# Feed-forward inner rows turned by 32x32 blocks on VectorE and gathered by transfers, in a two-block transformer kernel

## The reference

```python
def swiglu(h, w_gu, w_down):
    g, u = jnp.split(h @ w_gu, 2, axis=-1)
    return (jax.nn.silu(g) * u) @ w_down
```

## Time and profile before

| | us |
|---|---|
| median of three runs (1355.02 to 1355.81) | 1355.55 |
| span of the profiled execution, first to last instruction | 1354.2 |
| PE busy in it | 1339.0 |
| DVE busy | 930.6 |
| ACT busy | 749.4 |
| POOL busy | 67.2 |

### The profile page before, as it was taken

The page is one execution under the profiler, slowest core; times in us unless marked ns, Lnnn a source line. Parts: engine busy times, 40 slices in busy tenths (PEclk is TensorE's granted clock), DMA queues, the critical chain, the costliest instruction groups (busy, mean ns, idle before and its releaser), DMA issues.

```text
span 1354.2 us, 17190 instructions
## 1 busy us (share of the span) xinstructions
PE 1339.0 (99%) x6599; PEld 1117.7 (83%) x6599; DVE 930.6 (69%) x1334; ACT 749.4 (55%) x1169; POOL 67.2 (5%) x132
## 2 busy tenths in 40 slices
PE   9999999999999999999999999999999999999998
PEld 6888888888888888888788888889988888788886
DVE  6677867856656777877767787678866455755553
ACT  6444448567864544446845444766457664744442
POOL 3100100000000000010000010100000000000000
PEclk9999999999999999999999999999999999999999
DMA  9888866543376678885577885665544355556662
GB/s 282 290 262 277 310 199 190 167 117 108 100 243 195 214 252 272 289 288 167 168 245 250 279 290 150 202 173 159 168 140 112 108 172 169 166 180 184 187 190 88
DMA packets 167057, 270.89 MB, mean 200 GB/s; under 512 B 14242, under 2 KB 114826, under 8 KB 166976
## 3 DMA queue, kind: packets, MB, share of 16 engines
q1 hardware_dynamic: 154240, 226.66, 53.8%
q0 software_dynamic: 12576, 43.06, 9.5%
q10 hardware_dynamic: 160, 0.07, 0.0%
HBM read 268.66 MB, written 1.05 MB: 199 GB/s over the span
## 4 chain that ended last, share of the span: by engine, by line
PE 94%; DVE 3%; ACT 1%; DMA 1%; issue 0%; POOL 0%; DVEq 0%; SPq 0%; ACTq 0%
PE ps L1982 25%; PE ps L1947 16%; PE ps L1949 16%; PE ps L1948 16%; PE ps L2171 2%; PE ps L1961 1%; PE ps L2182 1%; PE ps L1962 1%; PE ps L1963 1%; PE ps L2065 1%; PE ps L2067 1%; PE ps L2066 1%; PE ps L2488 1%; PE ps L1997 1%; PE ps L2086 1%; PE ps L2255 1%
## 5 line engine op out<-in xcount | busy, mean ns | idle before, releaser
L1151 DVE TENSOR_TENSOR w_lo<-raw,w_hi 128x1024 fp32r<-128x1024 f32 (+2 forms) x431 | 515.1, 1214 | 249.1 <-ACT w_hi L636 246.9
L636 ACT ACTIVATE w_hi<-raw 128x1024 fp32r<-128x1024 f32 (+2 forms) x431 | 448.5, 1054 | 330.5 <-DMA raw<-in_ffn_wgu_dram 92.8
L1947 PE MATMUL ps<-w_hi,a_hi 128*128 128x512 f32 (+1 forms) x976 | 390.5, 400 | 1.1 <-DVE w_lo L1151 0.8
L1949 PE MATMUL ps<-w_hi,a_lo 128*128 128x512 f32 (+1 forms) x976 | 379.5, 389 | 0.0
L1948 PE MATMUL ps<-w_lo,a_hi 128*128 128x512 f32 (+1 forms) x976 | 378.5, 388 | 0.0
L1949 PEld LDWEIGHTS ps<-w_hi,a_lo 128*128 128x128 f32 x976 | 183.3, 188 | 38.8
L1947 PEld LDWEIGHTS ps<-w_hi,a_hi 128*128 128x128 f32 x976 | 183.6, 188 | 36.1 <-DVE w_lo L1151 1.0
L1948 PEld LDWEIGHTS ps<-w_lo,a_hi 128*128 128x128 f32 x976 | 183.8, 188 | 34.6
L1982 PE MATMUL ps<-w_hi,hid_hi 128*128 128x512 f32 x300 | 93.5, 393 | 0.0
L1982 PE MATMUL ps<-w_lo,hid_hi 128*128 128x512 f32 x300 | 92.5, 390 | 0.0
L1982 PE MATMUL ps<-w_hi,hid_lo 128*128 128x512 f32 x300 | 92.5, 390 | 0.0
(11 more groups left out here) (433 smaller groups left out, 1640.4 us busy)
## 6 DMA issues: line engine op xcount, KB each, us to landing
raw<-in_ffn_wgu_dram SPq DMA_DIRECT2D x176, 256.0 KB, 4.2
raw<-in_w_in_dram SPq DMA_DIRECT2D x88, 512.0 KB, 3.7
raw<-in_w_gu_dram SPq DMA_DIRECT2D x176, 256.0 KB, 3.3
ada<-in_w_ada_dram POOLq DMA_DIRECT2D x72, 512.0 KB, 5.4
raw<-in_ffn_wdown_dram SPq DMA_DIRECT2D x44, 512.0 KB, 4.6
raw<-in_w_dn_dram SPq DMA_DIRECT2D x44, 512.0 KB, 4.3
raw<-in_w_in_dram SPq DMA_DIRECT2D x36, 256.0 KB, 3.1
raw<-in_w_out_dram SPq DMA_DIRECT2D x16, 512.0 KB, 4.1
```

The source lines that it names most:

```text
L636: act.activation(w_hi[:, u % RING, 0:nk * n], raw[:, u % RING, 0:nk * n], ACT.Copy).then_inc(hi_ready, 1)
L1151: dve.tensor_tensor(w_lo[:, u % RING, 0:nk * n], raw[:, u % RING, 0:nk * n], w_hi[:, u % RING, 0:nk * n].bitcast(F32), ALU.subtract).then_ ...
L1947: pe.matmul(dst(t)[:, 0:n], a[0], slot(u, w_hi, kk, n), start=kc == 0, stop=False)
L1949: i = pe.matmul(dst(t)[:, 0:n], a[1], slot(u, w_hi, kk, n), start=False, stop=kc == KC - 1)
```

## The change

The four PE transposes of a block and their PSUM banks are gone. In their place three steps stand.

- DVE, right after it has made `hid` of a block (now one buffer, not two), transposes it within squares of 32x32 into a new tile `turned_blocks` (`turn_blocks`, two instructions of 128x256).
- After every second block SP issues 16 transfers from SBUF to SBUF, of 32 partitions x 2 x 128 floats (32 KB) each, which bring the squares to their partitions in `gathered` (`gather_hidden`). They stand in the queue that loads the weights, ahead of unit 4j+8 of the block j that comes next, and SP first waits there until both blocks are turned. A feed-forward part has 11 blocks, so there are 6 groups; the last one is for one block, with 16 transfers of half the size.
- ACT and DVE make `hid_hi` and `hid_lo` of two blocks at once from `gathered` (128x1024), after their units up to 4j+9 and just before the silu or `hid` of the even block j.

The diff, cut to its core:

```diff
+            def gather_hidden(f, m):
+
+                nh = 2 * min(2, UPB - 2 * m)
+                g = HGROUPS * f + m
+                sp.wait_ge(sem("blocks_turned"), f * UPB + min(2 * m + 2, UPB))
+                if g >= 1:
+                    sp.wait_ge(sem("hid_lo_ready"), g)
+                for i in range(4):
+                    for q in range(4):
+                        sp.dma_start(gathered[32 * q:32 * q + 32, :, i, 0:nh, :], turned_blocks[32 * i:32 * i + 32, :, q, 0:nh, :])\
+                          .then_inc(sem("hid_gathered"), 16)
+
+            gather_at = {}
+            for f in range(4):
+                for m in range(HGROUPS):
+                    gather_at[ffn[f][0] + 4 * min(2 * m + 2, UPB) + RING] = (f, m)
...
             for u in range(XQ, NU):
+                if u in gather_at:
+                    gather_hidden(*gather_at[u])
                 load_unit(u)
...
-                    if j >= 1:
-                        hidden_hi(f, j - 1)
                     if j < UPB - 1:
                         w.to(up + 4 * j + 8)
+                    if j >= 2 and j % 2 == 0:
+                        hidden_hi(f, j // 2 - 1)
...
-                w.to(dn + 5)
-                hidden_hi(f, UPB - 1)
+                w.to(dn + 8)
+                hidden_hi(f, HGROUPS - 1)
...
+            def hidden_hi(f, m):
+                n = 2 * min(2, UPB - 2 * m)
+                act.wait_ge(sem("hid_gathered"), 256 * (HGROUPS * f + m + 1))
+                act.activation(hid_hi[:, 4 * m:4 * m + n, :].rearrange("p c (g u) -> p c g u", u=32),
+                               gathered[:, :, :, 0:n, :].rearrange("p t i c u -> p c (t i) u"), ACT.Copy).then_inc(sem("hid_hi_ready"), 1)
...
+            def turn_blocks(f, j):
+
+                c = 2 * (j % 2)
+                dve.wait_ge(sem("hid_ready"), f * UPB + j + 1)
+                if j % 2 == 0 and f + j > 0:
+                    dve.wait_ge(sem("hid_gathered"), 256 * (HGROUPS * f + j // 2))
+                for t in range(T):
+                    i = dve.transpose(turned_blocks[:, t, :, c:c + 2, :], hid[:, t, :].rearrange("p (c q u) -> p q c u", c=2, u=32))
+                i.then_inc(sem("blocks_turned"), 1)
...
-            def turn_hidden(f, j):
-                pe.wait_ge(sem("hid_ready"), f * UPB + j + 1)
-                if j >= 2:
-                    pe.wait_ge(sem("hid_lo_ready"), f * UPB + j - 1)
-                for c in range(2):
-                    for t in range(T):
-                        i = pe.transpose(ps[:, 4 + j % 2, c * S + t * P:c * S + (t + 1) * P], hid[:, j % 2, t, c * P:(c + 1) * P], ident)
-                i.then_inc(sem("hid_turned"), 1)
```

More of the change, by code:

```diff
@@ L219, in two_blocks @@
         sg, _, e = place("sg", [P, 2, T, HALF], F32, HB)
-        hid, _, END = place("hid", [P, 2, T, HALF], F32, e)
+        hid, _, e = place("hid", [P, T, HALF], F32, e)
+        turned_blocks, _, END = place("turned_blocks", [P, T, 4, 4, 32], F32, e)
+        gathered, _, _ = place("gathered", [P, T, 4, 4, 32], F32, KD0)
         assert END <= nc.sbuf_usable_end, (END, nc.sbuf_usable_end)
@@ L417, in two_blocks @@
         FFN = ["f0", "f1", "f2", "f3"]
+        HGROUPS = (UPB + 1) // 2
         ROOTS = ["f2_1", "f2_post0", "mix2_0", "f2_post1", "mix2_1", "gla",
@@ L1390, in ffn_part @@
                 w.to(dn + 5)
-                hidden_lo(f, UPB - 1)
                 for n in range(4):
@@ L1395, in ffn_part @@
                     w.to(dn + 8 + 3 * n)
+                    if n == 0:
+                        hidden_lo(f, HGROUPS - 1)
                     if n == 1:
@@ L1402, in ffn_part, with hidden_lo @@
                 w.to(dn + FC + (1 if f == 2 else 2))
-            def hidden_lo(f, j):
-                dve.wait_ge(sem("hid_hi_ready"), f * UPB + j + 1)
-                dst, hf = (b[:, 2 * j:2 * j + 2, :].rearrange("p c n -> p (c n)") for b in (hid_lo, hid_hi))
-                dve.tensor_tensor(dst, ps[:, 4 + j % 2, :], hf.bitcast(F32), ALU.subtract).then_inc(sem("hid_lo_ready"), 1)
+            def turn_blocks(f, j):
[6 more added lines that the diff above has]
+                i.then_inc(sem("blocks_turned"), 1)
+            def hidden_lo(f, m):
+                n = 2 * min(2, UPB - 2 * m)
+                dve.wait_ge(sem("hid_hi_ready"), HGROUPS * f + m + 1)
+                dst, hf = (b[:, 4 * m:4 * m + n, :].rearrange("p c (g u) -> p c g u", u=32) for b in (hid_lo, hid_hi))
+                dve.tensor_tensor(dst, gathered[:, :, :, 0:n, :].rearrange("p t i c u -> p c (t i) u"), hf.bitcast(F32), ALU.subtract)\
+                   .then_inc(sem("hid_lo_ready"), 1)
             def ada_products(i0, n):
@@ L2128, in ffn_part @@
                             ins.then_inc(sem("par_turned"), 1)
-                        if j >= 1 and i == (2 if j == 1 else 1):
-                            turn_hidden(f, j - 1)
                         if i == 3:
```

27 lines of the change are left out of this document (10 added, 17 removed).

## The result

| | before | after |
|---|---|---|
| median, us | 1355.28 (1354.97 to 1355.81) | 1517.74 (1511.75 to 1519.57) |
| the profiled execution's own time, and its span | 1355.55, 1354.2 | 1511.75, 1509.9 |
| PE busy, and idle inside the span | 1339.0, 15.2 | 1361.4, 148.5 |

The ratio is 1.1191, 95% interval 1.1169 to 1.1213 (four runs of each, side by side). The prediction said slower, with 1404.5 us and a range of 1368 to 1440. The sign holds; the cost is 162 us, not 49, and outside the range.

What follows compares the result with a forecast made beforehand. PE was taken to bound the kernel, busy 1339.0 of 1354.2 us. Saving 20.7 us of transposes and adding waits of 22.4 us in each of f0 to f2 and 2.4 in f3 gave +48.9: 1404.5 us, range 1368 to 1440.

Steps and rivals of the forecast that it cites:

- 16 issues: SP's issuing of one group's transfers: 0.41 us each, 6.6 us in all, with bounds of 5.9 and 8.3 us.
- a ring through SP's queue: In f0 to f2, turned pair, issues, loads, conversions, `hid`, next turned pair: 26.3 us a turn, where PE needs 21.8.
- PE's transposes: On PE, removing the transposes of 44 blocks saves 0.47 us a block, 20.7 us in all.
- DVE's transposes and the conversions: On DVE and ACT: two transposes 0.85 us, `hid_lo` 1.2 and `hid_hi` 1.05 us for two blocks; double as upper end.
- the short form: On SP's queue, a gather transfer of 64 pieces of 512 B was expected to issue in 0.41 us.
- The landing: Weight loads behind the gather: data land 4.2 us after issue in f0 to f2, 3.3 us in f3.
- f3: Last feed-forward part: a turn 0.6 us too long, no block late, only a 2.4 us wait at the up half's end.
- The sum: Over the whole kernel: -20.7 + 3 x 22.4 + 2.4 = +48.9 us.
- The clock: Rival: new PE waits of 5 to 8 us bring TensorE to 1.2 GHz, 35 us more, 1440 us; chance 6%.
- the prediction's own sign of being wrong: On PE, a clock under 1 was listed among the observations that would show the forecast wrong; no size given.
- Dear issues: Rival: SP needs 0.52 us per issue, or runs of 32 slow ACT and DVE: 1439 us; chance 19%.
- The transfers don't overlap: Rival: each 32 KB transfer takes its own 2 us landing before the next, 32 us a group: near 1900 us; 2%.

Runs made afterwards that it cites:

- e13: Changed kernel with all gathers issued from GpSimd's queue, the sixth behind the part's vector loads, conversions and squares moved later on ACT and DVE: 1335.29 us, ratio 0.9859.
- e7: Kernel before the change, plus the 88 new DVE transposes written to a tile nobody reads: 1354.95 us, ratio 0.9994.
- e2: Changed kernel with a group's 16 transfers replaced by one of the same bytes, squares left on their partitions: 1338.03 us, ratio 0.9871.
- e1: Kernel before the change, plus 48 further transfers of several forms behind its last store; same form issued in 0.60 us from SBUF, 0.43 from HBM.
- e6: Changed kernel with 22 matmuls on dead data put before PE's waits at blocks 6, 8, 10 and in `first_down`: 1517.70 us, ratio 1.1200.

## Why the prediction was wrong

The step that failed is the term "16 issues": 0.41 us each and 6.6 us a group, bounds 0.37 and 0.52. The mechanism, a ring through SP's queue that is longer than PE's two blocks, was right; this term of it was mis-sized: 0.60 us each, 10.4 a group.

- **PE's transposes, 20.7 us: right.** e13 has PE busy 1317.8 us against 1339.0, 21.2 less, and is 20 us shorter.
- **DVE's transposes and the conversions: right.** Two transposes take 0.77 us in a row (0.85 said), `hid_lo` of 128x1024 1.22 and `hid_hi` 1.04, runs of 32 floats or not. e7 shows the transposes to be free, and e2 the rest.
- **The issue: mis-sized.** 0.60 us and 0.04 to the next, 10.2 to 11.7 us for a group (mean 10.4) where 6.6 were said and 8.3 was the upper bound. Each row that I bounded it by was a transfer out of HBM; e1 shows that the same form costs 0.17 us more out of SBUF. The argument "a quarter of the pieces, so the short form" was wrong in kind: in e1 the number of partitions counts 0.03. I should have kept a wider bound for a transfer of which no row showed the kind. In the turn shown the issues (10.55 us) make 4.0 of the 4.6 us by which it is longer than predicted.
- **The landing: a smaller miss.** Loads landed in 5.6 and 4.6 us, not 4.2 and 3.3; I took the old rows for loads that would now go out in a burst. With the loads' own issues (a unit now takes 1.0 us) this is about 1 us a turn.
- **f3: wrong with it.** Predicted at 0.6 us over PE's pace, it is the place where two small errors counted most: 27.1 to 28.9 us a turn, and 22 us of waits where 2.4 were said.
- **The sum.** PE's idle time grew by 133.3 us, where 3 x 22.4 + 2.4 = 69.6 were predicted. The four turns of the four parts took 489.3 us; the prediction has 4 x (26.3 x 3 + 22.4) and three times 2.5 for `fold_mods`, 412.7, so 77 us come from the turn's length alone. At the end of each up half the last whole group takes some 15 us from its turned pair to PE's work on `hid`, where 11.8 (f3: 11.6) were said, another 12 us in all.
- **Two waits I had not listed.** PE waits in the sum behind `fold_mods` (L2223, 29.5 us) and for the gate (L2219, 7.8 us). The first is not extra time: PE meets the late DVE there before it would at block 8's `hid`. I had put that wait before block 8.
- **The clock: wrong evidence, and then no price.** I argued from a stretch with a wait of 4.5 us in the chain and a full clock. But PE is busy 7.00 of 7.00 us in that very row; the wait was ACT's, and the row says nothing on a PE that idles. In the changed kernel PE idles 7.4 us before block 6 and is then granted half its clock (1.2 of 2.4 GHz): the prediction's own sign of being wrong, a clock under 1, came. Its busy time is 43 us longer than 1339.0 - 20.7. In an account by busy and idle time the span exceeds the predicted one by 107 us, 64 of them idle and 43 busy, which reads as if the clock cost 43. e6 speaks against that: with 22 of the 80 us at half clock gone, the turns and the time are the same. Most of the slower work lies inside the ring's waits; e6 doesn't show it for all.
- **The rivals.** "Dear issues", 1439 us at 0.52, was the right kind, at 19%. By the prediction's own steps 3.8 us more for a group, in 20 groups (five in each up half, since f3's ring has no slack left either), are 76 us: 1481. That is the size of what one duration did; of the other 37 us the trace shows the landings, some 1 us in each of 16 turns, and PE's wait for the gate, 7.8 us. The rest was not taken apart. "The transfers don't overlap" is refuted: 16 transfers are issued in 10.6 us, and the median one lands 1.9 us after its issue.

The Trainium skill, "DMA: Bandwidth & Descriptors", section "Rules for kernel authors", had spoken against many small transfers. e2 against the change agrees: the same bytes in one transfer (without the squares' change of partitions) are 180 us faster. What made the small ones dear was not their bandwidth or latency, it was their time on the issuing queue: e13 has the same 16 on another queue, with the order on ACT and DVE adapted, and is as fast as e2.

Left open: why an issue from SBUF to SBUF takes longer, what half the clock costs behind the last waits, and some 10 of the 107 us by which the span exceeds the predicted one (77 lie in the turns, 12 at the ends of the up halves, 8 at the gate).
